# Stick-breaking attention on one Trainium2 core: transposes taken singly between products instead of in runs

## What is computed

```python
z = jnp.einsum("bhqd,bhkd->bhqk", qb, kf) * scale
log_keep = jnp.where(mask, jax.nn.log_sigmoid(-z), 0.0)
later = lax.cumsum(log_keep, axis=3, reverse=True) - log_keep
log_a = jax.nn.log_sigmoid(z) + later
a = jnp.where(mask, jnp.exp(log_a), 0.0)
return jnp.einsum("bhqk,bhkd->bhqd", a, vf)
```

## Time and profile before

| | |
|---|---|
| median of 3 runs | 2880.52 us (2880.01 to 2880.65) |
| the profiled execution | 2882.65 us |
| its span, first to last instruction | 2881.0 us |
| PE busy | 2764.7 us, 96% of the span |
| DVE, ACT, POOL busy | 1452.7, 876.5, 292.5 us |
| mean granted clock of TensorE | 0.985 |
| the attention of layer 1 | about 1430 to 2014 us of the span |

### The profile page before, as it was taken

One profiled execution on the slowest core, in us unless ns is written; L12 is line 12 of the kernel. 1 busy time (PEld: TensorE's weight loads), 2 busy tenths in 40 slices (PEclk: granted clock), 3 DMA queues, 4 the chain that ended last, 5 costly groups with the idle time before them and its releaser, 6 DMA issues.

```text
span 2881.0 us, 35090 instructions
## 1 busy us (share of the span) xinstructions
PE 2764.7 (96%) x13160; PEld 2307.3 (80%) x13160; DVE 1452.7 (50%) x1845; ACT 876.5 (30%) x1369; POOL 292.5 (10%) x267
## 2 busy tenths in 40 slices
PE   7999999999999999999999989896999999999999
PEld 7888888888888888887877777775888888888887
DVE  7454434344444434454677777776334443444444
ACT  6450112231111111125656656564223111111110
POOL 2200000020000000003033333332001000000000
PEclk8999999999999999999999999997999999999999
DMA  5401111111111111113111101011311111111111
GB/s 198 139 30 44 58 44 52 44 44 51 44 44 58 44 51 44 50 45 117 59 29 30 30 29 29 23 32 59 129 51 44 44 44 58 51 44 44 51 51 66
DMA packets 41854, 158.35 MB, mean 55 GB/s; under 512 B 5552, under 2 KB 5552, under 8 KB 41392
## 3 DMA queue, kind: packets, MB, share of 16 engines
q1 hardware_dynamic: 34704, 124.83, 13.4%
q0 software_dynamic: 6784, 26.22, 2.7%
q10 hardware_dynamic: 288, 6.29, 0.5%
HBM read 138.98 MB, written 18.35 MB: 55 GB/s over the span
## 4 chain that ended last, share of the span: by engine, by line
PE 86%; issue 5%; DVE 3%; POOL 3%; ACT 2%; DMA 0%; POOLq 0%; SPq 0%; DVEq 0%; ACTq 0%
PE ps L1368 26%; PE ps L1370 26%; PE ps L1369 26%; POOL sig L486 3%; PE ps L1637 2%; PE ps L1596 1%; PE ps L1595 1%; ACT sig L706 1%; DVE w_lo L870 1%; DVE keep L1102 1%; PE ps L1469 1%; PE ps L1653 1%; PE ps L1498 0%; ACT keep L705 0%; DVE xg_lo L876 0%
## 5 line engine op out<-in xcount | busy, mean ns | idle before, releaser
L1368 PE MATMUL ps<-xg_hi,w_hi 128*128 128x512 f32 x2560 | 1015.4, 397 | 21.0 <-DVE tf L1118 7.5
L1370 PE MATMUL ps<-xg_hi,w_lo 128*128 128x512 f32 x2560 | 1002.1, 391 | 0.0
L1369 PE MATMUL ps<-xg_lo,w_hi 128*128 128x512 f32 x2560 | 1001.4, 391 | 0.0
L1368 PEld LDWEIGHTS ps<-xg_hi,w_hi 128*128 128x128 f32 x2560 | 483.6, 189 | 124.4 <-DVE tf L1118 9.6
L1370 PEld LDWEIGHTS ps<-xg_hi,w_lo 128*128 128x128 f32 x2560 | 483.1, 189 | 103.9
L1369 PEld LDWEIGHTS ps<-xg_lo,w_hi 128*128 128x128 f32 x2560 | 484.1, 189 | 94.9 <-issue 0.7
L529 ACT ACTIVATE w_hi<-raw 128x1024 fp32r<-128x1024 f32 x228 | 237.9, 1053 | 972.8 <-PE ps L1370 969.1
L870 DVE TENSOR_TENSOR w_lo<-raw,w_hi 128x1024 fp32r<-128x1024 f32 x228 | 290.6, 1282 | 299.4 <-ACT w_hi L529 295.1
L1306 DVE TENSOR_TENSOR x<-x,ps 128x512 f32<-128x512 f32 x352 | 235.6, 686 | 165.2 <-PE ps L1370 164.4
L1368 PE MATMUL ps<-act_hi,w_hi 128*128 128x512 f32 x704 | 277.3, 394 | 2.5 <-DVE x L1306 2.5
L1370 PE MATMUL ps<-act_hi,w_lo 128*128 128x512 f32 x704 | 276.0, 392 | 0.0
(11 more groups left out here) (176 smaller groups left out, 2803.5 us busy)
## 6 DMA issues: line engine op xcount, KB each, us to landing
raw<-wpack SPq DMA_DIRECT2D x228, 512.0 KB, 3.5
x<-xT POOLq DMA_DIRECT2D x2, 2048.0 KB, 13.0
d_x<-x POOLq DMA_DIRECT2D x1, 4096.0 KB, 17.7
x<-d_x ACTq DMA_DIRECT2D x1, 4096.0 KB, 18.1
out<-x SPq DMA_DIRECT2D x8, 512.0 KB, 2.6
d_mix<-o_sum POOLq DMA_DIRECT2D x56, 64.0 KB, 2.0
mx<-d_mix POOLq DMA_DIRECT2D x1, 3584.0 KB, 12.4
d_me<-me_f POOLq DMA_DIRECT2D x4, 512.0 KB, 2.9
```

The source lines that it names most:

```text
L1368: pe.matmul(out, whi, mhi, start=start, stop=False)
L1369: pe.matmul(out, whi, mlo, start=False, stop=False)
L1370: return pe.matmul(out, wlo, mhi, start=False, stop=stop)
```

## The change

Only PE's program is altered; no instruction is added or removed, and no buffer or semaphore is new.

1. In `weighted(c)` the transposes of chunk c+2, which came as a run after the four products, are now put singly after each product. `pv_done` is still signalled by the last product.
2. In items with t = 1 and 2 (`woven`) the turn of chunk 1 no longer follows that of chunk 0. Its 3 or 4 transposes are put singly after the products of the next item's first score row (`between`).

```diff
-                    def z(row, par, hh, r, t, first):
+                    def z(row, par, hh, r, t, first, between=None):
...
                             pe.matmul(o[:, 0:w], sq[:, slot, q], sk[:, slot, c:c + w], start=True, stop=False)
+                            if between:
+                                between(2 * c // HALF)
                             pe.matmul(o[:, 0:w], sq[:, slot, q], sk_lo[slot][:, c:c + w], start=False, stop=not final)
+                            if between:
+                                between(2 * c // HALF + 1)
...
+                        ahead = c + 2 if c + 2 <= t else None
                         for kk in range(2):
...
                             pe.matmul(o, v, aT_hi[:, n % 2, kk, cols], start=(c == 0 and kk == 0), stop=False)
+                            if ahead and 2 * kk < turns(it, ahead):
+                                turn_one(it, ahead, n + 2, 2 * kk)
                             last = pe.matmul(o, v, aT_lo[:, n % 2, kk, cols], start=False, stop=edge)
-                        last.then_inc(pv_done, 1)
+                            if kk == 1:
+                                last.then_inc(pv_done, 1)
+                            if ahead and 2 * kk + 1 < turns(it, ahead):
+                                turn_one(it, ahead, n + 2, 2 * kk + 1)
...
-                            for c in range(min(t + 1, 2)):
-                                turn(hp, it, c, par, first)
+                            woven = 1 <= t < 3
+                            turn(hp, it, 0, par, first)
+                            if t >= 1 and not woven:
+                                turn(hp, it, 1, par, first)
...
+                                    n = CHUNKS_BEFORE[it] + 1
+
+                                    def between(j):
+                                        if j == 0 and not (first and n < 2):
+                                            pe.wait_ge(aT_lo_ready, hp * CHUNKS + (n - 1))
+                                        if j < turns(it, 1):
+                                            turn_one(it, 1, n, j)
+
                                     z(hp * ROWS + (2 * (it + 1) + r), par, (it + 1) // 4, r, (it + 1) % 4,
-                                      False)
+                                      False, between if woven and r == 0 else None)
...
                                 weighted(hp, it, c, par, first)
-                                if c + 2 <= t:
-                                    turn(hp, it, c + 2, par, first)
```

More of the change, by code:

```diff
@@ L1625, in turn_values, with turns, turn_one @@
                         last.then_inc(vT_full, 1)
+                    def turns(it, c):
+                        return 3 if c == it % 4 else 4
+                    def turn_one(it, c, n, j):
+                        at = ((0, 0), (0, 1), (1, 1)) if c == it % 4 else ((0, 0), (0, 1), (1, 0), (1, 1))
+                        kk, r = at[j]
+                        k = 2 * c + kk
+                        last = pe.transpose(ps[:, 4 + n % 2, j * P:(j + 1) * P],
+                                            sig[:, it % 2, r, k * P:(k + 1) * P], ident[:])
+                        if j == len(at) - 1:
+                            last.then_inc(aT_full, 1)
                     def turn(hp, it, c, par, first):
@@ L1633, in turn @@
                             pe.wait_ge(aT_lo_ready, hp * CHUNKS + (n - 1))
[L1634 to L1639, removed]
+                        for j in range(turns(it, c)):
+                            turn_one(it, c, n, j)
                     def weighted(hp, it, c, par, first):
```

## The result

| | before | changed |
|---|---|---|
| median of 9 runs | 2880.74 us | 2886.21 us |
| ratio, 95% interval | | 1.0024 (1.0014 to 1.0033) |
| span of the profiled execution | 2881.0 us | 2883.9 us |

The changed kernel is slower by 0.24%, 6.9 us (4.0 to 9.5); the ratio is estimated without one slow execution of the kernel before (4621.74 us), and the two medians differ by 5.5 us. The time lies in the predicted range of 2869 to 2891 us, but the rise is not the 2.4 us that I had forecast, which nobody would measure. The profiled executions differ by only 2.9 us, since the attention, ahead of which nothing is changed, has its first sigmoid at 1427.12 us in the changed kernel and at 1430.77 in the kernel before. In all the traces of this document it lies between 1426.84 and 1430.78, so what follows compares stretches inside the attention.

The account below looks back on a forecast made before the run. PE was taken to bound the kernel, within a loop through ACT, DVE and POOL. Terms 1.1 + 0.4 + 0.9 = +2.4 us on the median 2880.52 gave 2882.9 us, range 2869 to 2891.

Parts of the forecast that it names:

- PE's price: On PE: a transpose costs about 0.12 us alone between products, against 0.11 or 0.116 in a run.
- +1.1 us: On PE: 224 transposes on the path, each 0.005 us dearer between products than in a run.
- A: On PE: weight loads hide under wide products, a transpose costs 0.06 us; faster, 2869.3 us; chance 0.22.
- C: On PE: each switch between transposes and products leaves a load uncovered; slower, 2903 us; chance 0.07.
- The value products: Later pv_done costs zero, since the copy waiting for it also waits for aT_full, and DVE is later.
- ACT's delay: Chunk 1's copy delays row 0's sigmoid by about 0.2 us in items 1 and 5, 0.45 in item 6.
- the ring: Attention loop: PE scores, ACT sigmoids, DVE scan, POOL product, PE transposes; 0.03 us reaches it in 14 items, +0.4 us.
- the 0.82 us of wait before item 7: PE's wait at item 7's transposes absorbs tf's 0.45 us delay in item 6, shrinking to about 0.4.
- the sign that I had set myself: Attention: the forecast is wrong if a head pair's 71.4 us differs by more than 0.5.
- Rival B: On ACT and DVE: chunk 1's copy delays row 0, and row 1's scan starts late; slower, 2888.9 us; chance 0.18.
- +0.9 us: Last pair, items 2 and 6: no fill between rows, so row 0's 0.45 us delay goes through in full.
- Same: Whole kernel: time within 0.2% of before, forecast's own range 2878 to 2886 us; chance 0.50, including no effect.

Follow-up runs that it names:

- POOL held back: Kernel before, with POOL's product of row 0 waiting until row 1 is scanned, items 0 to 6 of pairs 0 to 6; 2973.97 us in one execution.
- row 0 first in item 2: Kernel before, in item 2 alone: PE makes score row 0 before chunk 1's transposes, ACT and DVE take it before chunk 1's copies; 2875.82 us, ratio 0.9990.
- all four items: Kernel before, items 1, 2, 5, 6: PE makes score row 0 before chunk 1's transposes, ACT and DVE take it before chunk 1's copies; 2871.08 us, ratio 0.9971.

## Why the prediction was right or wrong

- **PE's price: right.** The forecast gave a transpose between products the price it has in a run, against the rival that its load would hide. It is 0.116 us in both. The +1.1 us that I added for a rise of 0.005 does not show. Rivals A and C fall with it: four transposes and four products take 0.93 us, where I had said 0.95, with 0.7 for A and above 1.2 for C. The value products, which I had put at nothing, cost nothing (71.27 us for pair 4).
- **ACT's delay: right in its size.** 0.19 us in items 1 and 5 (0.2 said), and in item 6 the sigmoid starts 2.46 us after the transposes instead of 1.99, 0.47 late (0.45 said). Item 2 keeps its 11.69 us, as said.
- **What the delay does: wrong, and this is the step that failed.** "Of the 0.2 some 0.03 reaches the ring" and "the 0.82 us of wait before item 7 cover it". I followed the row's results only to the next instruction on DVE and on PE, saw that the scan of row 1 kept its start, and took its duration for a constant. In item 6 PE did lose time waiting for `tf` (0.29 us), and yet its wait before item 7 stayed at 0.79 instead of shrinking to the 0.4 that I named, since POOL was later as well. POOL's product of row 0 was in my chain of engines but not in my rows. Of the 0.19 us all went through in items 1 and 5 (+0.19 each), and of the 0.47 in item 6 +0.27, about what is left after the 0.04 us between POOL's end and the scan and the 0.14 of overlap that costs nothing: 0.65 us a pair, 4.6 us in pairs 0 to 6, where I had 0.4. By the sign that I had set myself, a pair's time moved by more than 0.5 us, the forecast was wrong.
- **Rival B** had the right engines, delay and sign, with 2888.9 us a little above what came; but it put the mechanism at the wrong place. It asked whether the scan would start late, and decided at DVE's idle time of 0.21 us. The scan never started late, so by the sign set for B, a scan that moves, B would have been turned down although its size was nearly right.
- **The sum.** 4.6 us of the measured 6.9 (4.0 to 9.5) are accounted for by items 1, 5 and 6, in pairs 0 to 6. Between the first sigmoid of pair 0 and that of the last pair the profiled executions differ by 6.3 us (1430.77 to 1937.34, and 1427.12 to 1940.00). Pairs 0, 1, 2, 4 and 6 are longer by 0.63 to 0.71 each, pairs 3 and 5 by 2.1 and 0.9. In both PE stops once, before item 1's transposes, for 2.6 to 2.9 us, in every trace here but that with POOL held back, where such waits are many. What causes it stays open. What the granted clock does after it differs from trace to trace: in the trace before it was 1.00 in the ten microseconds around pair 3's stop,

```profile
1658.00:1668.00 10.00, 6.61 (x39) 5.51 (x37) 7.84 (x9) 5.47 (x10) 4.90 (x4) 1.00 0.16 61
```

and in the changed kernel's 0.83.

```profile
1656.00:1666.00 10.00, 7.09 (x33) 5.91 (x32) 6.10 (x8) 4.38 (x8) 4.26 (x3) 0.83 0.20 61
```

- The remainder of 1.7 us I leave to these two pairs without a proof that the change has no part in it. Pair 3 is longer than pair 4 by 2.2 us in the trace before and by 3.6 in the changed kernel, but also by 3.4 and 3.8 with row 0 first in item 2 and in all four items, where the score rows are not woven. For the last pair I had +0.9 us; from its first sigmoid to the start of the output projection's operands the two traces have 78.6 and 78.5 us, and those of the two halves of the change 76.6 and 77.5. That scatter is wider than the term, no run tests it by itself, and it stays open.
- **The chances.** "Same" had 0.50, "slower" 0.27. The interval of the result, 0.14% to 0.33%, contains the 0.2% that I took as the border, so it does not tell which of the two came. The sign was right, the size a third. That the time lies in the range of 2869 to 2891 us is luck as far as the mechanism goes: the range reached so far up for the sake of B, and B named another path than the one that acted.

## What to carry to other kernels

A duration in a trace can hold a wait inside. Compare the same instruction at the same shape in several places (1024 columns: 2.29 and 2.73 us) before calling it a constant, and look for who runs beside the longer one. If it is VectorE with two inputs in SBUF and GpSimd reading SBUF, count the earlier one's end as what releases the other. And when a queue is reordered, ask first which row the slow chain needs soonest: here moving transposes cost and gave nothing on PE, while moving the row that feeds scan and product ahead of chunk 1's transposes and copies gave 7 us.

## What the runs showed of the hardware that I had not expected

- VectorE's scan over `keep` (inputs and output in SBUF) and GpSimd's product of `sig` and `keep` exclude each other: with 0.30 to 0.80 us of overlap the scan lasts longer by the overlap less 0.14 us. GpSimd's instruction, being first, kept its time (1.31 or 1.32 us for 639 columns in every one of these cases, 1.76 or 1.77 for 895); being second, it took 1.91 us instead of 1.54 for 767.
- The blocked time stands inside the instruction's duration. No idle time and no wait of the profile shows it.
- 128-column transposes put between products of 256 columns hide nothing: the eight cost 0.116 us each, though each successor's start is recorded 0.03 us after the transpose. The load of that successor begins with the transpose and not earlier (1516.30 us, the transpose at 1516.29, in the score row of the changed kernel), which fits one weight load being ahead and no more.
